# Inner feed-forward groups with the weight block stationary, and the row factor multiplied in by VectorE

## The chip, the cores and the metric

The kernel runs on one core of one Trainium2 chip. The metric is the device time of one execution in microseconds; the number given is the median over several runs. TensorE (PE in the profile) multiplies, ScalarE (ACT), VectorE (DVE) and GpSimd (POOL) do the elementwise work, and SyncE (SP) issues the transfers of the weights.

## The reference, cut to what matters

Three transformer blocks for 256 tokens with a model width of 1024, all in float32. The part that is changed is their feed-forward layers: four gated ones with an inner width of 2816, and one of another form with an inner width of 4096.

```python
def rms_norm(x, g):
    xf = x.astype(jnp.float32)
    y = xf * lax.rsqrt(jnp.mean(xf * xf, axis=-1, keepdims=True) + EPS)
    return (y * g.astype(jnp.float32)).astype(x.dtype)

def swiglu(h, w_gate, w_up, w_down):
    return (jax.nn.silu(h @ w_gate) * (h @ w_up)) @ w_down

# twice in each of the two layers of the first part (ffn0 to ffn3):
f = swiglu(rms_norm(x, g[0]), w_ffn_gate[layer, 0], w_ffn_up[layer, 0], w_ffn_down[layer, 0])
x = x + 0.5 * rms_norm(f, g[1])

# at the end of the second part (ff):
hn = rmsnorm(h, norm2_g[l])
h = h + jnp.square(jax.nn.relu(hn @ w_ff1[l])) @ w_ff2[l]
```

## The kernel before

**Three products for one.** The matmuls run in the type fp32r. Each operand is split in two parts, a rounded one (hi) and the remainder (lo), and a product is the sum of three matmuls: hi by hi, hi by lo, lo by hi (`mm3`, lines 573 to 577; the profile names these lines L575, L576 and L577). The 1.05 MB pieces of the weights arrive in four buffers `raw0` to `raw3` (SP, line 487). ScalarE writes `whi` (L1538) and VectorE writes `wlo` (L2155) from each of them; `used` tells that TensorE has read a piece for the last time, and so when its slot may be overwritten.

**x.** A normalisation is not applied to x: x is transposed unscaled except for the gain (which belongs to the rows of the weights), and lies as `xh` and `xl`, eight tiles of 128 rows by 256 tokens each. The factor of each token, 1/rms, is put in where sums are read out: as the tokens lie on the partitions there, it is a value per partition (`rcol`), which ScalarE's activation and VectorE's instruction take as their scale.

**Groups.** A gated layer is worked in 11 groups (`steps`) of 256 inner columns. The weights of the first product of a group are 512 columns, 256 of the gate and 256 of the up part, in two pieces `e0` and `e1` (the upper and the lower four tiles of 128 rows). In `x_half` a block of 128 tokens of `xh` or `xl` is the stationary operand and the 512 weight columns move past it: 8 tiles by 2 token blocks by 3 = 48 matmuls of 512 columns, with the sums in the two PSUM banks `GU`. ScalarE takes the silu of the gate part (L1649), VectorE multiplies by the up part (L2272) and writes `hid`, tokens on the partitions. The second product needs `hid` with its columns on the partitions, so TensorE transposes it (`hidden_transposes`, L768, 4 blocks of 128 by 128, float32) into the PSUM bank `TB`, from where ScalarE writes `hth` (L1638) and VectorE `htl` (L2265). The second product (`down`) is 2 tiles by 2 token blocks by 2 halves by 3 = 24 matmuls of 512 columns, added up in the four banks `DD`. The last layer, `ff`, has 8 groups of 512 inner columns; its sums go through relu (L1652) and a square (L2277), its transposes are 8, and its second product 48 matmuls.

**Order.** The order on every engine is written out by hand. On TensorE step g (function `step`, line 787) is: first half of the first product of group g, the transposes of group g-1, second half of the first product, second product of group g-1. ScalarE and VectorE do in the same step: the split of the second product's weights, `hth`/`htl` of group g-1, the split of `e0` of group g+1, the activation and product of group g, the split of `e1` of group g+1. Group 0 is done by token blocks in `head` (`first_head` in `ffn0`), the last group in `tail` or `tail2`, also by token blocks, so that their results are complete early. The groups between, 9 in each gated layer and 6 in `ff`, are called the inner groups here. Before step 1 of `ffn0` ScalarE also waits for two transposes of small parameters (L1498, L1499), which TensorE does in the middle of that step (`other_columns`).

Of the kernel before, what the change touches and what calls it, by code (L numbers as in the profile page):

```python
# [21 lines left out]
F32 = mybir.dt.float32  # L22
# [29 lines left out]
R_GKV, R_N1, R_N2, R_LB = 96, 104, 112, 120  # L52
R_PEK, R_PEV, R_SUB, R_HG, N_SM2 = 24, 40, 56, 57, 58
# [138 lines left out]
def two_blocks(nc, a, out, stop=None):  # L192
    ctx = ExitStack()
    with ctx:
# [14 lines left out]
        xh = sb("xh", [P, KT, S], F32R)  # L209
        xl = sb("xl", [P, KT, S], F32R)  # L210
# [55 lines left out]
        cols_ready = sem("cols_ready")  # L266
        out_ready, out_done, scaled, end_ready = sem("out_ready"), sem("out_done"), sem("scaled"), sem("end_ready")
# [44 lines left out]
        class Places:  # L312


            def __init__(self):
                self.next, self.gu, self.d, self.t, self.xh, self.hth = 0, 0, 0, [0, 0], 0, 0
                self.d0, self.x, self.h = 0, 0, 0
                self.gu0 = 0
# [10 lines left out]
        psc = sb("psc", [P, 2, 3 * P])  # L329
        lamv = small[:, 0:256].rearrange("p (i d) -> p i d", i=4)  # L330
# [238 lines left out]
        def _(pe):  # L569
# [179 lines left out]
            def ffn(name):  # L749
                steps, nd = ffn_shape(name)  # L750
                per, base, gu0 = 2 + nd, n.next, n.gu
# [3 lines left out]
                def hidden_ready(g, t, d=0):  # L755
                    if nd == 1:
                        pe.wait_ge(gu_used[t], d + gu0 + g + 1)
                    else:
                        pe.wait_ge(h_ready[t], d + sq0 + g + 1)

                def hidden_transposes(g, d):

                    for t in range(TT):
                        hidden_ready(g, t, d)
# [6 lines left out]

                def down(g, es, d, start):

                    for b, e in enumerate(es):
                        pe.wait_ge(t_used[b], d + t0[b] + g + 1)
# [11 lines left out]
                def step(g, at, d=0, static=True):  # L787

                    es = ent[at:at + per]
# [6 lines left out]
                    if name == "ffn0" and static and g == 1:  # L796
# [3 lines left out]
                    if name == "ffn0" and static and g == 1:  # L800
# [3 lines left out]
                def tail_transposes(g, t):  # L804

                    hidden_ready(g, t)
# [16 lines left out]
                def gate_tail(g, e0, e1):  # L823

                    for t in range(TT):
                        pe.wait_ge(gu_used[t], gu0 + g)
                    pe.wait_ge(lo_done[e0.slot], e0.raw_before + 1)
                    x_rows(gu_banks[0], e0, 0, 0)
                    hidden_transposes(g - 1, 0)
# [4 lines left out]
                def tail(g, at):  # L834
                    e0, e1, d0, d1 = ent[at:at + 4]
                    gate_tail(g, e0, e1)
                    pe.wait_ge(t_used[0], t0[0] + g)
                    tail_transposes(g, 0)
                    down_rows(d0, 0, 0)
                    pe.wait_ge(t_used[0], t0[0] + g + 1)  # L840
# [3 lines left out]
                    tail_transposes(g, 1)  # L844
                    down_rows(d0, 0, 1, range(1, 2)).then_inc(used[d0.slot], 1)
                    pe.wait_ge(t_used[1], t0[1] + 1)
                    n.t = [t0[0] + steps, t0[1] + 1]
# [6 lines left out]
                def tail2(g, at):  # L854
                    e0, e1, *ds = ent[at:at + 6]
                    gate_tail(g, e0, e1)
                    x_rows(gu_banks[1], e1, 1, 1).then_inc(used[e1.slot], 1)
                    for t in range(TT):
                        pe.wait_ge(t_used[t], t0[t] + g)
                    for t in range(TT):  # L860
# [4 lines left out]
                        tail_transposes(g, t)  # L865
                    for t in range(TT):
                        pe.wait_ge(t_used[t], t0[t] + g + 1)
# [2211 lines left out]
```

## Time and profile before

| what | value |
|---|---|
| time, median of 3 runs | 1379.26 us (1378.42 to 1379.76) |
| the profiled execution, first to last instruction (its span) | 1377.0 us |
| PE busy | 1359.0 us, 99% of the span, 6525 matmuls |
| PEld (weight loads) busy | 1116.0 us |
| DVE busy | 815.2 us, 59% |
| ACT busy | 681.7 us, 50% |
| POOL busy | 41.7 us, 3% |
| transfers | 247.09 MB, mean 179 GB/s |

The profile is of one execution on the chip. Its own time isn't printed beside its span; the median of the timed runs lies 2.3 us above the span, which is what lies around the first and the last instruction. The start of a row is more telling than its duration for TensorE, since matmuls overlap and their ends are modelled: the distance from one start to the next is what a matmul costs in a stream. A row of the timeline gives the start in us, the duration in us, engine, line, operation, output and inputs, the form and how many instructions were merged, and in brackets the idle time before and what ended it.

### The profile page before, as it was taken

The page shows a single profiled execution, that of the slowest core. Times are in us where ns is not written, and L with a number is a line of the kernel's source. Part 1 is how long each engine was busy: PE and PEld are TensorE (multiplying, and loading weights), DVE is VectorE, ACT ScalarE, POOL GpSimd, SP SyncE. Part 2 cuts the span into 40 slices and gives each one's busy share as a digit, 9 for nine tenths or more (in the row PEclk, how much of TensorE's full clock was granted, in tenths as well). Part 3 has the DMA queues.
Part 4 walks back from the last instruction along what each step waited for, and adds up shares of the span by engine and source line. Part 5 has one row for each costly group of instructions (what it writes and reads, how often), then busy time and mean ns, then how long its engine had stood idle before and what let it go on. Part 6 is the DMA issues. An engine that isn't in the chain of part 4 may idle for free.

```text
span 1377.0 us, 17411 instructions
## 1 busy us (share of the span) xinstructions
PE 1359.0 (99%) x6525; PEld 1116.0 (81%) x6525; DVE 815.2 (59%) x899; ACT 681.7 (50%) x875; POOL 41.7 (3%) x112
## 2 busy tenths in 40 slices
PE   8999999999999999999999999999999999999997
PEld 6888888888888888888887788888878778888886
DVE  5545567665555655554568855555767668654553
ACT  5444454464444554444467644444664466544442
POOL 3000000000000000000000100000000000000000
PEclk9999999999999999999999999999999999999999
DMA  8655656455556554655653265557444354565540
GB/s 294 210 192 191 222 166 217 159 165 193 185 183 215 197 183 139 192 188 183 230 182 108 93 199 193 188 183 240 163 178 153 104 175 141 191 219 190 178 166 31
DMA packets 160381, 247.09 MB, mean 179 GB/s; under 512 B 9103, under 2 KB 104649, under 8 KB 160329
## 3 DMA queue, kind: packets, MB, share of 16 engines
q1 hardware_dynamic: 160216, 246.33, 54.0%
q8 instruction: 35, 0.57, 0.2%
q14 instruction: 18, 0.14, 0.0%
q10 hardware_dynamic: 112, 0.05, 0.0%
HBM read 245.30 MB, written 1.05 MB: 179 GB/s over the span
## 4 chain that ended last, share of the span: by engine, by line
PE 97%; DVE 1%; ACT 1%; issue 0%; DMA 0%; POOL 0%; POOLq 0%; ACTq 0%; DVEq 0%
PE GU L575 15%; PE GU L577 15%; PE GU L576 15%; PE DD L575 12%; PE DD L577 12%; PE DD L576 12%; PE GU L640 4%; PE TB L612 3%; PE GU L647 2%; PE TB L768 2%; PE DD L1208 0%; PE GU L1473 0%; PE TB L1224 0%; PE GU L1476 0%; PE GU L1467 0%
## 5 line engine op out<-in xcount | busy, mean ns | idle before, releaser
L2155 DVE TENSOR_TENSOR wlo<-raw,whi 128x2048 fp32r<-128x2048 f32 x224 | 509.3, 2282 | 268.5 <-ACT whi L1538 268.3
L1538 ACT ACTIVATE whi<-raw 128x2048 fp32r<-128x2048 f32 x223 | 423.8, 1906 | 175.8 <-PE DD L577 167.9
L575 PE MATMUL GU<-whi,xh 128*128 128x512 f32 x928 | 367.3, 396 | 0.0
L577 PE MATMUL GU<-whi,xl 128*128 128x512 f32 x928 | 362.1, 390 | 0.0
L576 PE MATMUL GU<-wlo,xh 128*128 128x512 f32 x928 | 361.2, 389 | 0.0
L577 PEld LDWEIGHTS GU<-whi,xl 128*128 128x128 f32 x928 | 174.2, 188 | 37.3
L575 PEld LDWEIGHTS GU<-whi,xh 128*128 128x128 f32 x928 | 174.2, 188 | 35.4 <-issue 1.1
L576 PEld LDWEIGHTS GU<-wlo,xh 128*128 128x128 f32 x928 | 174.5, 188 | 34.5
L575 PE MATMUL DD<-whi,hth 128*128 128x512 f32 x496 | 194.8, 393 | 0.0
L577 PE MATMUL DD<-whi,htl 128*128 128x512 f32 x496 | 193.2, 390 | 0.0
L576 PE MATMUL DD<-wlo,hth 128*128 128x512 f32 x496 | 193.0, 389 | 0.0
L1638 ACT ACTIVATE hth<-TB 128x512 fp32r<-128x512 f32 x54 | 31.6, 599 | 165.0 <-PE TB L768 165.0
L577 PEld LDWEIGHTS DD<-whi,htl 128*128 128x128 f32 x496 | 93.1, 188 | 19.6
L576 PEld LDWEIGHTS DD<-wlo,hth 128*128 128x128 f32 x496 | 93.2, 188 | 18.8
L575 PEld LDWEIGHTS DD<-whi,hth 128*128 128x128 f32 x496 | 93.1, 188 | 18.7
L1649 ACT ACTIVATE sg<-GU,rs 128x256 f32<-128x256 f32 x88 | 41.8, 475 | 113.3 <-PE GU L577 106.5
L575 PE MATMUL DD<-whi,xh 128*128 128x512 f32 (+1 forms) x240 | 93.8, 391 | 0.1
L577 PE MATMUL DD<-whi,xl 128*128 128x512 f32 (+1 forms) x240 | 92.0, 383 | 0.0
L576 PE MATMUL DD<-wlo,xh 128*128 128x512 f32 (+1 forms) x240 | 92.0, 383 | 0.0
L2265 DVE TENSOR_TENSOR htl<-TB,hth 128x512 fp32r<-128x512 f32 x54 | 36.7, 690 | 89.8 <-ACT hth L1638 89.8
L2272 DVE SCALAR_TENSOR_TENSOR hid<-GU,rs,sg 128x256 f32<-128x256 f32 x88 | 42.3, 481 | 41.3 <-ACT sg L1649 41.2
L575 PEld LDWEIGHTS DD<-whi,xh 128*128 128x128 f32 x240 | 45.1, 188 | 9.1 <-DVE wlo L2155 0.5
(304 smaller groups left out, 1069.6 us busy)
## 6 DMA issues: line engine op xcount, KB each, us to landing
raw<-in_w_ffn_down SPq DMA_DIRECT2D x88, 512.0 KB, 4.2
raw<-in_w_ffn_gate SPq DMA_DIRECT2D x86, 512.0 KB, 4.0
raw<-in_w_ffn_up SPq DMA_DIRECT2D x86, 512.0 KB, 4.9
raw<-in_w_ff SPq DMA_DIRECT2D x64, 512.0 KB, 4.3
raw<-in_w_in SPq DMA_DIRECT2D x40, 512.0 KB, 4.5
raw<-in_w_conv_in SPq DMA_DIRECT2D x24, 512.0 KB, 4.8
raw<-in_w_kv SPq DMA_DIRECT2D x16, 512.0 KB, 4.8
raw<-in_w_conv_out SPq DMA_DIRECT2D x8, 512.0 KB, 4.7
```

What stands on the lines that cost most here:

```text
L575: pe.matmul(dst, h, w_h, start=start, stop=False)
L576: pe.matmul(dst, h, w_l, start=False, stop=False)
L577: return pe.matmul(dst, l, w_h, start=False, stop=stop)
L612: mm = pe.transpose(TB[0:m, bank, c:c + r], src, ident[0:r, 0:r])
L640: pe.matmul(dst[:, 0:m], xh[:, 4 * half + k, ts], view(w[e.slot], e)[:, k, :], start=(half == 0 and k == 0 and w is whi), stop=False)
L647: mm = pe.matmul(dst[:, 0:m], xl[:, 4 * half + k, ts], view(whi[e.slot], e)[:, k, :], start=False, stop=(half == 1 and k == 3))
L1538: nc.scalar.activation(whi[s][:, 0:size], raw[s][:, 0:size], ACT.Copy).then_inc(hi_done[s], 1)
L1638: nc.scalar.activation(hth[:, 2 * b:2 * b + 2, :].rearrange("p k n -> p (k n)"), TB[:, b, :], ACT.Copy).then_inc(hth_done[b], 1)
L1649: nc.scalar.activation(sg[:, t, 0:FG], GU[:, t, 0:FG], ACT.Silu, scale=rcol(pre, t)).then_inc(sg_done[t], 1)
L2155: nc.vector.tensor_tensor(wlo[s][:, 0:size], raw[s][:, 0:size], whi[s][:, 0:size].bitcast(F32), ALU.subtract).then_inc(lo_done[s], 1)
L2265: nc.vector.tensor_tensor(htl[:, 2 * b:2 * b + 2, :].rearrange("p k n -> p (k n)"), TB[:, b, :], hth[:, 2 * b:2 * b + 2, :].rearrange("p k ...
L2272: nc.vector.scalar_tensor_tensor(out=hid[:, t, 0:FG], in0=GU[:, t, FG:512], scalar=rcol(pre, t), in1=sg[:, t, 0:FG], op0=ALU.mult, op1=ALU ...
```

## The change

The first product of an inner group is turned round: a block of 128 rows by 128 weight columns is stationary, and x moves. `xh` and `xl` now lie in one tensor `xx`, so that one matmul of 512 columns has both parts of x move past a `whi` block (sums with xh in the first 256 columns of a bank, with xl in the other 256), and a second one of 256 columns has `xh` alone move past the `wlo` block, added to the first 256 columns. The sums come out with the inner columns on the partitions, so the transposes of these groups go. The four blocks of 128 columns fill four banks: `GU` (called pair 0, the gate) and now `TB` too (pair 1, the up part). `hidden_hi` and `hidden_lo` read `hid` instead of `TB` from group 1 on. ScalarE copies the xl halves of a pair to SBUF, VectorE adds the xh halves, multiplies by the row factor (now a value per column, so a row `rrow` that is the same on all partitions is needed), ScalarE takes the silu of pair 0 and VectorE makes the product. The row is made once for each layer: GpSimd spreads the factors over 128 columns (`rcols`), TensorE transposes these (`row_factors`), ScalarE copies the result. Group 0 and the last group stay as they are, except that fewer waits are needed.

```diff
-        xh = sb("xh", [P, KT, S], F32R)
-        xl = sb("xl", [P, KT, S], F32R)
+        xx = sb("xx", [P, 2, KT, S], F32R)
+        xh, xl = xx[:, 0, :, :], xx[:, 1, :, :]
...
+        def pair_of(p):
+            return (GU, TB)[p][:, :, :].rearrange("p a (u n) -> p a u n", u=2)
+        def both(t):
+            return t.rearrange("p (a n) -> p a n", a=2)
...
+                def row_factors():
+                    pe.wait_ge(rb_ready, n.rows + 1)
+                    for t in range(TT):
+                        mm = pe.transpose(DD[:, 2, t * P:(t + 1) * P], rcols[:, t, :], ident[:, :])
+                    mm.then_inc(row_t, 1)
+                def inner_part(e, half, pair, free=None):
+                    wh, wl = view(whi[e.slot], e), view(wlo[e.slot], e)
+                    for j in range(2):
+                        if free:
+                            pe.wait_ge(free[j], gu0 + 1)
+                        dst, cs = (GU, TB)[pair][:, j, :], slice((2 * pair + j) * P, (2 * pair + j + 1) * P)
+                        for k in range(4):
+                            kk = 4 * half + k
+                            pe.matmul(both(dst), wh[:, k, cs], xx[:, :, kk, :], start=(half == 0 and k == 0), stop=False)
+                            mm = pe.matmul(dst[:, 0:S], wl[:, k, cs], xh[:, kk, :], start=False, stop=(half == 1 and k == 3))
+                    return mm
-                    if g == 1:
-                        x_half(gu_banks, es[0], 0, 0, False, read=(gu_used, gu0 + 1), rows=True)
-                    else:
-                        for t in range(TT):
-                            pe.wait_ge(gu_used[t], d + gu0 + g)
-                        x_half(gu_banks, es[0], 0, 0, False, d=d)
-                    hidden_transposes(g - 1, d)
-                    x_half(gu_banks, es[1], 1, 4, True, d=d, done=gu_ready)
-                    down(g - 1, es[2:], d, start=(static and g == 1))
+                def step_1(at):
+                    e0, e1, *ds = ent[at:at + per]
+                    pe.wait_ge(lo_done[e0.slot], e0.raw_before + 1)
+                    inner_part(e0, 0, 0, gu_used)
+                    if name == "ffn0":
+                        other_columns()
+                    row_factors()
+                    first_transposes()
+                    pe.wait_ge(lo_done[e1.slot], e1.raw_before + 1)
+                    inner_part(e1, 1, 0).then_inc(w_ready, 1)
+                    for b in range(nd):
+                        pe.wait_ge(t_used[b], t0[b] + 1)
+                    inner_part(e0, 0, 1).then_inc(used[e0.slot], 1)
+                    inner_part(e1, 1, 1).then_inc(used[e1.slot], 1)
+                    pe.wait_ge(row_ready, n.rows)
+                    down(0, ds, 0, True)
+                def step(g, at, d=0):
+                    e0, e1, *ds = ent[at:at + per]
+                    pe.wait_ge(w_used[0], d + w0 + g - 1)
+                    pe.wait_ge(lo_done[e0.slot], d + e0.raw_before + 1)
+                    inner_part(e0, 0, 0)
+                    pe.wait_ge(w_used[1], d + w0 + g - 1)
+                    inner_part(e0, 0, 1).then_inc(used[e0.slot], 1)
+                    pe.wait_ge(lo_done[e1.slot], d + e1.raw_before + 1)
+                    inner_part(e1, 1, 0).then_inc(w_ready, 1)
+                    inner_part(e1, 1, 1).then_inc(used[e1.slot], 1)
+                    down(g - 1, ds, d, False)
...
+                def inner_low_sums(p, g, d):
...
+                    nc.scalar.activation(both(sg[:, p, :]), pair_of(p)[:, :, 1, :], ACT.Copy).then_inc(w_copied[p], 1)
+                def inner_gate(g, d):
+                    act.wait_ge(w_scaled[0], d + w0 + g)
+                    nc.scalar.activation(sg[:, 0, :], hid[:, 0, :], ACT.Silu).then_inc(w_gate, 1)
                     split(ent[e + nd], d)
-                    gate(g, d)
+                    inner_low_sums(0, g, d)
+                    if nd == 1:
+                        inner_gate(g, d)
+                    inner_low_sums(1, g, d)
                     split(ent[e + nd + 1], d)
...
+                def inner_sums(p, g, d):
...
+                    nc.vector.tensor_tensor(both(hid[:, p, :]), pair_of(p)[:, :, 0, :], both(sg[:, p, :]), ALU.add)\
+                        .then_inc(w_used[p], 1)
+                def inner_scales(p, g, d):
+                    nc.vector.tensor_tensor(both(hid[:, p, :]), both(hid[:, p, :]), rrow.unsqueeze(1).broadcast_to([P, 2, S]),
+                                            ALU.mult).then_inc(w_scaled[p], 1)
+                def inner_products(g, d):
+                    if nd == 1:
+                        nc.vector.tensor_tensor(hid[:, 0, :], hid[:, 1, :], sg[:, 0, :], ALU.mult).then_inc(w_hid[0], 1)
+                        return
+                    for p in range(2):
+                        nc.vector.scalar_tensor_tensor(out=hid[:, p, :], in0=hid[:, p, :], scalar=0.0, in1=hid[:, p, :],
+                                                       op0=ALU.max, op1=ALU.mult).then_inc(w_hid[p], 1)
                     split(ent[e + nd], d)
-                    hidden(g, d)
+                    inner_sums(0, g, d)
+                    inner_scales(0, g, d)
+                    inner_sums(1, g, d)
+                    inner_scales(1, g, d)
+                    inner_products(g, d)
                     split(ent[e + nd + 1], d)
...
+                nc.gpsimd.tensor_copy(rcols, rs[:, c:c + TT].unsqueeze(2).broadcast_to([P, TT, P])).then_inc(rb_ready, 1)
```

## Rows read from the trace of the kernel before

**Rows 1.** The page, busy time of each engine.
```profile
PE 1359.0 (99%) x6525; PEld 1116.0 (81%) x6525; DVE 815.2 (59%) x899; ACT 681.7 (50%) x875; POOL 41.7 (3%) x112
```
**Rows 2.** The page, the chain that ended last, by engine.
```profile
PE 97%; DVE 1%; ACT 1%; issue 0%; DMA 0%; POOL 0%; POOLq 0%; ACTq 0%; DVEq 0%
```
**Rows 3.** The waits of PE, the longest: sum, times, longest one.
```profile
PE DD L1503 <- DMA proj<-in_g_norm: 4.4, 1, 4.4
```
**Rows 4.** Windows: one inner step of ffn0, then no matmul at the end.
```profile
56.00:72.79 16.79, 16.79 (x78) 13.91 (x77) 8.45 (x6) 7.08 (x7) 0.00 (x0) 1.00 0.57 187
...
1370.00:1373.00 3.00, 0.00 (x0) 0.00 (x0) 2.28 (x3) 1.15 (x2) 0.59 (x2) 1.00 0.40 165
1373.00:1374.00 1.00, 0.00 (x0) 0.00 (x0) 0.55 (x1) 0.62 (x1) 0.14 (x1) 0.54 0.00 0
```
**Rows 5.** Timeline of PE around the transposes of an inner step of ffn0.
```profile
60.91 0.40 PE L577 MATMUL GU<-whi,xl 128*128 128x512 f32 x1
61.15 0.60 PE L768 MATMUL TB<-ident,hid 128*128 128x128 f32 x4
...
61.82 0.39 PE L576 MATMUL GU<-wlo,xh 128*128 128x512 f32 x1
```
**Rows 6.** The same in ff.
```profile
1226.81 0.40 PE L577 MATMUL GU<-whi,xl 128*128 128x512 f32 x1
...
1228.15 0.39 PE L576 MATMUL GU<-wlo,xh 128*128 128x512 f32 x1
```
**Rows 7.** Timeline of PE: fp32r matmuls of 280 columns, nine starts.
```profile
1128.06 0.29 PE L575 MATMUL DD<-whi,xh 128*128 128x280 f32 x1
...
1129.08 0.29 PE L577 MATMUL DD<-whi,xl 128*128 128x280 f32 x1
```
**Rows 8.** Timeline: four fp32r matmuls of 256 columns and their followers.
```profile
728.79 0.50 PE L1000 MATMUL DD<-hth 64*128 64x256 f32 x4 [0.25 <-ACT proj L1770]
...
729.14 0.82 PE L1004 MATMUL DD<-proj 64*128 64x128 f32 x7
```
**Rows 9.** Lines of PE: the transposes of hid.
```profile
L768 PE MATMUL TB<-ident,hid 128*128 128x128 f32 x216 | 31.2, 272 | 0.0
```
**Rows 10.** The page, costliest groups, two of DVE.
```profile
L2155 DVE TENSOR_TENSOR wlo<-raw,whi 128x2048 fp32r<-128x2048 f32 x224 | 509.3, 2282 | 268.5 <-ACT whi L1538 268.3
...
L2265 DVE TENSOR_TENSOR htl<-TB,hth 128x512 fp32r<-128x512 f32 x54 | 36.7, 690 | 89.8 <-ACT hth L1638 89.8
```
**Rows 11.** Timeline, ffn1: first matmul of step 1, last product of group 0.
```profile
301.70 0.39 PE L575 MATMUL GU<-whi,xh 128*128 128x512 f32 x1
...
303.27 0.48 DVE L2272 SCALAR_TENSOR_TENSOR hid<-GU,rs,sg 128x256 f32<-128x256 f32 x1
```
**Rows 12.** The same in ffn2, then in ffn3.
```profile
536.54 0.39 PE L575 MATMUL GU<-whi,xh 128*128 128x512 f32 x1
...
537.25 0.48 DVE L2272 SCALAR_TENSOR_TENSOR hid<-GU,rs,sg 128x256 f32<-128x256 f32 x1
...
795.23 0.39 PE L575 MATMUL GU<-whi,xh 128*128 128x512 f32 x1
...
796.73 0.48 DVE L2272 SCALAR_TENSOR_TENSOR hid<-GU,rs,sg 128x256 f32<-128x256 f32 x1
```
**Rows 13.** The same in ffn0, with the split of its first down weights and htl.
```profile
21.59 0.39 PE L575 MATMUL GU<-whi,xh 128*128 128x512 f32 x1
...
23.66 0.48 DVE L2272 SCALAR_TENSOR_TENSOR hid<-GU,rs,sg 128x256 f32<-128x256 f32 x1
...
27.78 1.92 ACT L1538 ACTIVATE whi<-raw 128x2048 fp32r<-128x2048 f32 x1
...
31.93 0.68 DVE L2265 TENSOR_TENSOR htl<-TB,hth 128x512 fp32r<-128x512 f32 x1
```
**Rows 14.** The same in ff: first matmul of step 1, and both htl.
```profile
1198.91 0.39 PE L575 MATMUL GU<-whi,xh 128*128 128x512 f32 x1
...
1206.05 1.28 DVE L2265 TENSOR_TENSOR htl<-TB,hth 128x512 fp32r<-128x512 f32 x2
```

More of the change, by code:

```diff
@@ L52 @@
 R_GKV, R_N1, R_N2, R_LB = 96, 104, 112, 120
+FFNS = ("ffn0", "ffn1", "ffn2", "ffn3", "ff")
 R_PEK, R_PEV, R_SUB, R_HG, N_SM2 = 24, 40, 56, 57, 58
@@ L266, in two_blocks @@
         cols_ready = sem("cols_ready")
+        rb_ready, row_t, row_ready = sem("rb_ready"), sem("row_t"), sem("row_ready")
+        w_ready, w_gate = sem("w_ready"), sem("w_gate")
+        w_copied, w_used, w_scaled, w_hid, w_low = ([sem(f"{x_}{i}") for i in range(2)] for x_ in (
+            "w_copied", "w_used", "w_scaled", "w_hid", "w_low"))
         out_ready, out_done, scaled, end_ready = sem("out_ready"), sem("out_done"), sem("scaled"), sem("end_ready")
@@ L317, in __init__ @@
                 self.d0, self.x, self.h = 0, 0, 0
-                self.gu0 = 0
+                self.w, self.rows = 0, 0
         def ffn_shape(name):
@@ L821, in down_rows, with gate_tail @@
                     return mm
-                def gate_tail(g, e0, e1):
-                    for t in range(TT):
-                        pe.wait_ge(gu_used[t], gu0 + g)
+                def gate_tail(e0, e1):
+                    pe.wait_ge(w_used[0], w0 + steps - 2)
                     pe.wait_ge(lo_done[e0.slot], e0.raw_before + 1)
                     x_rows(gu_banks[0], e0, 0, 0)
-                    hidden_transposes(g - 1, 0)
                     pe.wait_ge(lo_done[e1.slot], e1.raw_before + 1)
@@ L1630, in ffn @@
                 steps, nd = ffn_shape(name)
-                per, t0, gu0 = 2 + nd, list(n.t), n.gu
+                per, t0, gu0, w0 = 2 + nd, list(n.t), n.gu, n.w
+                n.rows += 1
                 base = seg[name]
@@ L1716, in ffn @@
                     hidden_hi(steps - 2, 0)
-                    gate(steps - 1, 0)
+                    for t in range(TT):
+                        gate_rows(1, t)
                     split(ent[e + 2])
@@ L2258, in ffn @@
                 steps, nd = ffn_shape(name)
-                per, gu0, sg0, hth0 = 2 + nd, n.gu, n.sg, n.hth
+                per, gu0, sg0, hth0, w0 = 2 + nd, n.gu, n.sg, n.hth, n.w
+                n.rows += 1
                 base = seg[name]
@@ L2333, in ffn @@
                     hidden_lo(steps - 2, 0)
-                    hidden(steps - 1, 0)
+                    for t in range(TT):
+                        dve.wait_ge(w_low[t], n.w if t == 0 else steps - 2)
+                        hidden_rows(1, t)
                     split(ent[e + 2])
@@ L3007, in norms, with row_columns @@
                     norm(1, ssq[:, c:c + 1], msq[:, c:c + 1], rs[:, c:c + 1], D, rs_ready)
+            def row_columns(name):
+                pre = {"ffn0": "pre0", "ffn1": "pre2", "ffn2": "pre4", "ffn3": "pre6", "ff": "pre8"}[name]
+                pool.wait_ge(rs_ready, order(pre))
+                c = ncol[pre]
+                if name != "ffn0":
+                    pool.wait_ge(row_t, FFNS.index(name))
+                nc.gpsimd.tensor_copy(rcols, rs[:, c:c + TT].unsqueeze(2).broadcast_to([P, TT, P])).then_inc(rb_ready, 1)
             chain(nc.gpsimd.memset(ident[:, :], 0.0))
@@ L3043, in _ @@
             ins.then_inc(const2, 1)
-            norms("pre0", "pre5")
+            norms("pre0", "pre0")
+            row_columns("ffn0")
+            norms("post0", "pre2")
+            row_columns("ffn1")
+            norms("post2", "pre3")
+            row_columns("ffn2")
+            norms("post3", "pre5")
             pool.wait_ge(rs_ready, order("pre5"))
```

170 lines of the change are left out of this document (98 added, 72 removed).

## The prediction

> **What bounds the kernel now.** I read the page's busy times first. TensorE is busy for 1359.0 us, 99% of the span, VectorE for 59%, ScalarE for 50% [rows 1]. A busy share near one isn't proof, so the chain that ended last comes next: 97% of it is TensorE [rows 2]. The waits say the same from the other side: the longest that TensorE ever had was 4.4 us for the first transfer [rows 3], and no wait inside a feed-forward layer is listed. The windows then give one inner step of a gated layer, 16.79 us, with TensorE busy throughout, VectorE for 8.45 and ScalarE for 7.08 us, transfers at 57%, the granted clock at 1.00 [rows 4]. So the kernel is a stream of matmuls. What the change is worth is read from distances between starts on TensorE, and only there, unless it makes TensorE wait.
>
> **Prices on TensorE.** An inner step has 72 matmuls of 512 columns and one block of four transposes. From the last matmul before the block to the second one behind it are 0.91 us [rows 5]. Two distances of plain matmuls lie in that. If one is w, then 72 w + (0.91 - 2 w) = 16.79, so w = 0.227 us, and the block costs 0.46 us. In ff the same two starts are 1.34 us apart [rows 6], so its block of eight costs 1.34 - 0.45 = 0.89. The difference, 0.43 for four more, puts one transpose at 0.108 us.
>
> The matmul of 256 columns is what decides. No full-height one in fp32r is in the trace. The nearest rows are those of 280 columns: nine starts, so eight distances, in 1.02 us, 0.1275 us each [rows 7]. Between 280 and 512 columns a column costs (0.227 - 0.1275) / 232 = 0.43 ns, so 256 columns come to 0.1275 - 24 x 0.00043 = 0.117 us. A second row bears it out: four fp32r matmuls of 256 columns on two halves of the rows, so two in sequence on each half, take 0.35 us from the first load to the start of the next kind [rows 8]. With one exposed load of about a transpose's distance taken off, 0.12 us each are left. I take 0.118. Bounds: not under 0.108, the distance of a transpose with its own load of 128 columns, and not over 0.1275, that of 280 columns.
>
> The Trainium skill (TensorE: Matmul & The Clock Gate, section "Back-to-back issue gap") has N / 2.4 + 2.5 ns for a warm matmul, 109 ns for 256 columns. For 512 columns it gives 216 ns, and the distance of 227 here says that it leaves out 11 ns in this stream [rows 5]; by its figure for 256 alone my forecast would be 12 us lower. The same page (section "LDWEIGHTS (loading the stationary operand)") has P / 1.2, 107 ns for a block of 128 columns. That speaks against the change: the loads are 64 for each first product instead of 48, and half of them have only a 256-column matmul to hide behind. By this rule it still fits into 118 ns, by 11.
>
> **What goes.** Of the 216 transposes of hid in `hidden_transposes` [rows 9] those of group 0 stay. Gone are nine blocks of 0.46 us in each of four layers, 16.6 us, and six of 0.89 in ff, 5.3 us. Sum: -21.9 us.
>
> **What comes on TensorE.** Two transposes for the row of factors in each of five layers, 10 x 0.108 = +1.1 us. The first product of an inner group is 32 matmuls of 512 columns and 32 of 256 instead of 48 of 512: the same number of columns, but sixteen more starts. There are 4 x 9 + 6 = 42 inner groups: 1344 x 0.118 - 672 x 0.227 = 158.6 - 152.5 = +6.1 us. By the bounds of the 256-column matmul this term is -7.4 to +18.9. That the moving operand now has two pieces far apart I cost at nothing: the matmuls of [rows 8] read a repeated operand in two pieces.
>
> **What comes on VectorE and ScalarE.** Per gated step VectorE loses 0.69 + 2 x 0.48 and gains hidden_lo from SBUF, two sums, two scalings and one product of 512 columns, each taken as the htl row, 0.69 [rows 10]: 3 x 2.28 + 6 x 0.69 = 11.0 us of a step of 16.5. I followed the order through a step that starts at 0. Split of the down weights done at 4.4, htl at 5.1; e0 is released at 5.52 and split until 9.9; pair 0 of the sums is complete at 8.28, read out and added by 10.6, scaled 11.3; pair 1, complete at 11.04, is added by 13.2, scaled 13.9, product 14.6, split of e1 until 16.8. TensorE wants pair 0's banks at 16.5, pair 1's at 19.2, the split e1 at 22.0, and htl of this group at 27.5. Every slack is over 5 us, so both engines stay hidden, at a cost of nothing. If each elementwise pass took twice 0.69, e1 would still be 1 us early. In ff VectorE has 4 x 2.28 + 8 x 0.69 = 14.6 of 21.9 us. Transfers move the same bytes, the weight buffers come free at nearly the same points, and the transfers of such a step take 57% of their engines' time [rows 4]. The row itself: GpSimd's copy starts once the factors are there, some 5 us before TensorE gets to it, and it has 3% to do [rows 1]. ScalarE's copy of it is 0.2 to 0.7 us in a slack of 5 us.
>
> **What comes as waits.** Step 1 of each layer has a new order, and this is where I expect TensorE to stand still.
> - Bank j = 1 of `GU` is wanted 6 distances earlier: after half of pair 0's first part, 4 x (0.227 + 0.118) = 1.38 us from the step's start, instead of 2.72. It comes free when group 0's second product ends on VectorE, plus some 0.06 us for the signal. In ffn1: free at 303.27 + 0.48 + 0.06 = 303.81, wanted at 301.70 + 1.38 = 303.08, a wait of 0.7 [rows 11]. In ffn2 537.79 against 537.92, none; in ffn3 797.27 against 796.61, 0.7 [rows 12]. In ffn0 24.20 against 22.97, 1.2 [rows 13]. In ff ScalarE frees it, early enough. Together 2.6 us.
> - `TB` is now a bank for sums. Pair 1 of step 1 may start only when htl of group 0 has been made from it. Before, that was due at the second product, two quarters later. In ffn0 pair 1 is reached at 24.20 + 1.38 + 0.4 (parameters) + 0.22 (row) + 0.46 + 2.76 = 29.4, and htl ends at 31.93 + 0.68 = 32.6 [rows 13], since the split of the down weights, begun at 27.78 behind the parameter columns, comes first on both engines. TensorE gets to the columns 1.5 us earlier than before, so if the weights had landed the wait would shrink by that; the transfers of this stretch are dense, and I take them as landing about when the split began. Wait: 3.2 (bounds 1.6 and 3.2). In ff it is reached at 1198.91 + 2.76 + 0.22 + 0.89 + 2.76 = 1205.5, and the second htl ends at 1206.05 + 1.28 = 1207.4 [rows 14], behind two splits in VectorE's queue: 1.9. In ffn1 to ffn3 one split stands ahead and htl is done about a microsecond early. Together 5.1 us.
> - No clock is lost: at the end the granted clock is at 1.00, 2.4 GHz, through 3 us with no matmul at all, and falls in the next slice [rows 4]. The longest wait is 3.2 us. If it did fall, the stretch behind would run at 1.2 GHz, and some 2 to 3 us more would go.
> - In the tail the transposes of the last group come 0.46 us earlier. VectorE then has two splits, htl and the product to do in 8.2 us, which by the durations above ends at 7.6. Nothing, at most 0.5 us in each layer.
>
> **Sum.** -21.9 + 1.1 + 6.1 + 2.6 + 5.1 = -7.0 us. The profiled span of 1377.0 becomes 1370; the median lies 2.3 us above its span, so 1379.3 becomes 1372.3.
>
> **Rivals.**
> - A, the waits don't come, because group 0's work on VectorE and ScalarE moves forward with TensorE: only the steady terms stay, -14.7, 1364.6 us. Against it: the products and the splits that are waited for hang on the head and on transfers, which don't change.
> - B, the 256-column matmul runs at its lower bound: 1344 x 0.010 less, 1358.9 us with the waits. For it: transposes load as many columns in 0.108. Against it: [rows 8] and the line through 280 and 512.
> - C, slower than before: the 256-column matmul is bound by the weight load ahead of it and goes no faster than the 280-column one. At 0.1275, 1344 x 0.0095 = 12.8 more, 1385.1 us. The point from which it decides is 0.118 + 7.0 / 1344 = 0.123 us, halfway between my value and the bound. For it: no row has 256 full-height columns in fp32r, and loads take turns with matmuls of two lengths. If a load really held TensorE for the 0.171 us that its busy time comes to (1116.0 / 6525 [rows 1]), it would be 1344 x 0.053 = +71 us, but 280 columns at 0.1275 exclude that.
> - D, the change doesn't hide where it should: VectorE's chain is longer than I have it and holds back pair 0's banks in each of 42 groups. A quarter microsecond in each would be +10, 1383. Against it are 5 us of slack.
>
> **Chances.** The forecast with its own spread (1368 to 1376.5) 0.52; A 0.12; B 0.08; C 0.15; D or another new wait 0.05; in between forecast and C, with a matmul at 0.121 to 0.124 or longer waits, 0.08. A measurement of this kernel tells a difference from none at about 0.2%, 2.8 us. Faster by more: the first three, 0.72. Within it: 0.12. Slower: 0.16. The range reaches from A, 1363, to 1383, short of C: below lies most of B, above about half of C.
>
> **What would show it.** In the profile after: starts of the first product alternate between 0.227 and 0.118 us; an inner step of a gated layer takes 16.5 us against 16.79, one of ff 21.9 against 22.7; the 192 transposes of hid are gone; PE's waits list VectorE at step 1 of ffn0 and ff with about 3 and 2 us; VectorE is busy for some 110 us more. Wrong would be a distance above 0.123 behind a 256-column matmul, a wait in every inner step, or a granted clock below 1.00 after 32 us.

## The result and the profile after

| | before | after |
|---|---|---|
| median of the timed runs | 1379.46 us (1378.42 to 1379.76, 4 runs) | 1386.83 us (1386.15 to 1387.81, 4 runs) |
| span of the profiled execution | 1377.0 us | 1384.3 us |
| time of that execution | not printed | 1386.2 us |

The changed kernel is slower: the ratio after to before is 1.0056 [1.0044, 1.0068]. The forecast was 1372.3 us and its range ended at 1383, so the forecast missed by 14.5 us and had the wrong sign. Between the spans lie +7.3 us where I had -7.0.

The page after, busy time of each engine, answers to [rows 1]. Below it stands the chain that ended last, answering to [rows 2].

```profile
PE 1359.5 (98%) x7015; PEld 1133.5 (82%) x7015; DVE 912.4 (66%) x1031; ACT 710.1 (51%) x916; POOL 44.1 (3%) x117
...
PE 94%; DVE 2%; ACT 2%; SPq 1%; DMA 1%; issue 0%; POOL 0%; POOLq 0%; ACTq 0%; DVEq 0%
```

The kernel is still a stream of matmuls, and VectorE got its 97 us (110 forecast) without leading the chain. PE's busy time is the number to stop at: 192 transposes have gone, worth 21.9 us, and it did not fall (1359.0 to 1359.5). Something in the stream costs as much as they did.

The waits of PE after (sum, times, longest) answer to [rows 3]. The first is the old one for the first transfer.

```profile
PE DD L1558 <- DMA proj<-in_g_norm: 4.4, 1, 4.4
PE TB L803 <- DVE htl L2345: 4.2, 2, 2.5
PE GU L803 <- DVE hid L2351: 2.1, 3, 1.0
...
PE GU L1522 <- DVE whi L3061: 1.1, 1, 1.1
```

The rows of L803 are the two new waits of step 1, 6.3 us, where I had 5.1 and 2.6.

Next, one inner step of ffn0. This row of the windows after answers to the first of [rows 4].

```profile
79.54:96.33 16.79, 16.79 (x89) 14.30 (x88) 10.76 (x10) 7.88 (x7) 0.00 (x0) 1.00 0.58 187
```

The step takes 16.79 us, as before, not 16.5. There is no wait in it, the clock is at 1.00, and the transfers take 58% (57% before). So in the steady state of a gated layer the change gives nothing, though a block of 0.46 us has gone from each step. In ff, where the block that goes is 0.89 us, it gives something. The windows between two starts of the second product there are, before and after:

```profile
1233.40:1256.09 22.69, 22.69 (x105) 18.84 (x104) 11.76 (x9) 9.91 (x8) 0.00 (x0) 1.00 0.56 186
...
1243.45:1265.69 22.24, 22.24 (x115) 18.82 (x113) 14.17 (x13) 9.80 (x8) 0.00 (x0) 1.00 0.57 189
```

That is 0.45 us a step, where 0.8 was forecast. The timeline of PE inside the step of ffn0 shows why. This is the first product of the inner group, which answers to [rows 5].

```profile
79.88 0.40 PE L803 MATMUL GU<-xx,whi 128*128 128x512 f32 x1
80.11 0.28 PE L804 MATMUL GU<-xx,wlo 128*128 128x256 f32 x1
80.23 0.40 PE L803 MATMUL GU<-xx,whi 128*128 128x512 f32 x1
80.47 0.28 PE L804 MATMUL GU<-xx,wlo 128*128 128x256 f32 x1
...
80.94 0.40 PE L803 MATMUL GU<-xx,whi 128*128 128x512 f32 x1
```

From 79.88 to 80.94 are three pairs in 1.06 us, 0.353 us a pair. My sum had 0.227 + 0.118 = 0.345. A pair divides into 0.117 (0.11 to 0.12) behind the start of the short matmul, as forecast, and 0.236 (0.23, then 0.24) behind the start of the long one, which I had left at 0.227. So the excess shows beside the short matmul and not on it.

It also outlasts the group. The second product behind it, which the change doesn't touch, starts like this in the kernel after:

```profile
74.04 0.40 PE L589 MATMUL DD<-whi,hth 128*128 128x512 f32 x1
74.28 0.40 PE L590 MATMUL DD<-wlo,hth 128*128 128x512 f32 x1
74.52 0.40 PE L591 MATMUL DD<-whi,htl 128*128 128x512 f32 x1
74.75 0.40 PE L589 MATMUL DD<-whi,hth 128*128 128x512 f32 x1
```

These distances are 0.24, 0.24 and 0.23; after about ten matmuls they are back at 0.227, and 0.06 us has been lost by then. From 74.04 to the next step's start at 79.54 the second product takes 5.50 us, 24 x 0.2267 + 0.06. Of the 16.79 that leaves 11.29 for the 32 pairs of the first product, 0.3528 each, as the three pairs above say.

Where the time went over the whole kernel:

| term | forecast | found after |
|---|---|---|
| transposes of hid gone | -21.9 | -21.9 |
| row of factors, 10 transposes | +1.1 | +1.1 |
| first product: 1344 pairs at 0.3528 less 2016 x 0.2267 | +6.1 | +17.1 |
| second product, its first matmuls late, 42 x 0.061 | 0 | +2.6 |
| waits for `GU` and for htl | +7.7 | +6.3 |
| clock at half behind the wait in ffn0 | 0 | +1.6 |
| step 1 of ffn0 begins later | 0 | +1.0 |
| sum | -7.0 | +7.8 (measured +7.3) |

The two transposes of a row take 0.22 us up to the next kind's start, as priced (0.28 in ffn0). The clock's term is five pairs that took 3.35 us (33.25 to 36.60) instead of 1.76. The later start of step 1 in ffn0 (22.58 instead of 21.59) has two parts in the timelines: the wait ahead of the head's first matmul of 512 columns grew from 0.54 to 1.08, and such matmuls followed each other at 0.425 us, as the half clock gives, until 12.5 us instead of 11.1, which costs another 0.4. The sum is 0.5 us above what was measured; that part I can't place.

### The profile page after: what moved, and what is told of

The parts are those of the page before. It is cut to its first block, busy times and chain, and to the rows that moved or that the text cites. A ratio compares the mean times of both kernels' runs of the same rounds, so it can differ in the third digit from the quotient of the medians.

```text
span 1384.3 us, 18651 instructions
## 1 busy us (share of the span) xinstructions
PE 1359.5 (98%) x7015; PEld 1133.5 (82%) x7015; DVE 912.4 (66%) x1031; ACT 710.1 (51%) x916; POOL 44.1 (3%) x117
## 4 chain that ended last, share of the span: by engine, by line
PE 94%; DVE 2%; ACT 2%; SPq 1%; DMA 1%; issue 0%; POOL 0%; POOLq 0%; ACTq 0%; DVEq 0%
PE DD L589 12%; PE DD L591 12%; PE DD L590 12%; PE TB L803 11%; PE GU L803 11%; PE TB L804 6%; PE GU L804 5%; PE GU L589 4%; PE GU L591 4%; PE GU L590 4%; PE GU L654 4%; PE TB L626 3%; PE GU L661 2%; DVE wlo L2232 1%; ACT whi L1593 1%; DMA raw<-in_w_ffn_down 1%
## 5 line engine op out<-in xcount | busy, mean ns | idle before, releaser
L803 PE MATMUL TB<-xx,whi 128*128 128x512 f32 x672 | 242.4, 400 | 4.2 <-DVE htl L2345 4.2
L803 PE MATMUL GU<-xx,whi 128*128 128x512 f32 x672 | 241.3, 399 | 2.1 <-DVE hid L2351 2.1
L804 PE MATMUL TB<-xx,wlo 128*128 128x256 f32 x672 | 189.3, 282 | 0.0
L804 PE MATMUL GU<-xx,wlo 128*128 128x256 f32 x672 | 188.8, 281 | 0.0
L803 PEld LDWEIGHTS TB<-xx,whi 128*128 128x128 f32 x672 | 127.0, 189 | 36.4 <-DVE htl L2345 4.8
L803 PEld LDWEIGHTS GU<-xx,whi 128*128 128x128 f32 x672 | 126.2, 188 | 33.1 <-DVE hid L2351 3.0
L804 PEld LDWEIGHTS GU<-xx,wlo 128*128 128x128 f32 x672 | 126.9, 189 | 1.6
L804 PEld LDWEIGHTS TB<-xx,wlo 128*128 128x128 f32 x672 | 127.8, 190 | 0.0
L589 PE MATMUL GU<-whi,xx 128*128 128x512 f32 x256 | 101.1, 395 | 0.0
L591 PE MATMUL GU<-whi,xx 128*128 128x512 f32 x256 | 99.9, 390 | 0.0
L589 PE MATMUL DD<-whi,xx 128*128 128x512 f32 (+1 forms) x240 | 93.9, 391 | 0.0
L591 PE MATMUL DD<-whi,xx 128*128 128x512 f32 (+1 forms) x240 | 92.1, 384 | 0.0
```

Of the source, the lines that this page charges most:

```text
L589: pe.matmul(dst, h, w_h, start=start, stop=False)
L591: return pe.matmul(dst, l, w_h, start=False, stop=stop)
L803: pe.matmul(both(dst), wh[:, k, cs], xx[:, :, kk, :], start=(half == 0 and k == 0), stop=False)
L804: mm = pe.matmul(dst[:, 0:S], wl[:, k, cs], xh[:, kk, :], start=False, stop=(half == 1 and k == 3))
```

## The experiments

The expectations name four theories of the 0.353 us. **L** (layout): the moving operand, read from two pieces 2048 columns (8 KB) apart, is slow by itself. **R** (rhythm): the change between two lengths costs it as such. **S** (short slot): a matmul of 256 columns can't quite cover the load of 128, and a run of short ones would show that on themselves. **K**, from e5 on: the load that falls into the short slot comes late, and the lateness is passed on to the long matmuls behind. All diffs are against the changed kernel. "Step" is the distance between the starts of the second product in successive inner steps of ffn0 (16.79 in the kernel after).

**e1, the two parts of x side by side.**

```diff
-xx = sb("xx", [P, 2, KT, S], F32R)
-xh, xl = xx[:, 0, :, :], xx[:, 1, :, :]
+xx = sb("xx", [P, KT, 2, S], F32R)
+xh, xl = xx[:, :, 0, :], xx[:, :, 1, :]
...
-pe.matmul(both(dst), wh[:, k, cs], xx[:, :, kk, :], ...)
+pe.matmul(both(dst), wh[:, k, cs], xx[:, kk, :, :], ...)
```

> The changed kernel with xx laid out [P, KT, 2, S], so that the moving operand of the 512-column matmul is one contiguous piece. In the changed kernel a pair of a 512- and a 256-column matmul takes 0.353 us (0.236 + 0.117) where 0.345 was forecast. Theory L (layout: a moving operand of two pieces 8 KB apart costs 10 ns at each 512-column matmul): the pair falls to 0.344, 1344 pairs, 12 us less, 1375 us. Rival R (rhythm: matmuls of two lengths in turn cost it, whatever the layout): the pair stays at 0.353 and the time at 1387 us.

Measured: 1384.42 us (1383.77 to 1386.12), ratio 1.0041 [1.0027, 1.0055]. The timeline of PE in e1, the same place in a step:

```profile
79.15 0.40 PE L803 MATMUL GU<-xx,whi 128*128 128x512 f32 x1
...
80.21 0.40 PE L803 MATMUL TB<-xx,whi 128*128 128x512 f32 x1
```

Three pairs lie between these two rows, again in 1.06 us, and the step is 16.79. Theory L falls. The 2.4 us between the two medians are no more than what differs in ffn0: the wait for htl was 1.7 us instead of 2.5, the clock didn't fall there (1.6), and the wait for whi was 0.6 instead of 1.1.

**e2, the short matmuls in runs of four.**

```diff
 for k in range(4):
     pe.matmul(both(dst), wh[:, k, cs], xx[:, :, 4 * half + k, :], ...)
+for k in range(4):
     mm = pe.matmul(dst[:, 0:S], wl[:, k, cs], xh[:, 4 * half + k, :], ...)
```

> The changed kernel with the matmuls of each block of 128 columns in another order: the four of 512 columns one after the other, then the four of 256. Theory R: the cost sits at the change of length, eight changes in eight matmuls become two, so the 512-column distance falls to about 0.227 to 0.230 and three quarters of 12 us go: 1378 us. Rival S (the short matmul: a 256-column slot can't quite cover the load of 128 columns and its issue, and the backlog shows at its neighbour): four in a row show it openly as a distance of about 0.126, and the sum and the time stay, 1387 us. Theory L: the 512-column distance stays at 0.236, 1387 us.

Measured: 1381.09 us (1380.26 to 1382.14), ratio 1.0012 [1.0003, 1.0022]; the step is 16.69. The timeline of PE in e2, where a row with x4 is a run of four:

```profile
78.86 1.09 PE L802 MATMUL GU<-xx,whi 128*128 128x512 f32 x4
79.79 0.63 PE L804 MATMUL GU<-xx,wlo 128*128 128x256 f32 x4
80.26 1.09 PE L802 MATMUL TB<-xx,whi 128*128 128x512 f32 x4
```

From 78.86 to 79.79 four long ones take 0.93 (0.2325 each), and from 79.79 to 80.26 four short ones 0.47 (0.1175 each). The same matmuls in another order save 0.1 us a step, so the price isn't a constant of either kind of matmul. But it doesn't sit at the changes of length alone either. At 0.2267 and 0.117 throughout, the step would be 16.44. With a quarter of the changes 0.25 of the 0.35 us above that are left, where R had counted on a quarter (1378 us), and S's 0.126 in a run of four doesn't appear.

**e3, no short matmul.** It adds the term low times low to the inner groups.

```diff
-mm = pe.matmul(dst[:, 0:S], wl[:, k, cs], xh[:, kk, :], ...)
+mm = pe.matmul(both(dst), wl[:, k, cs], xx[:, :, kk, :], ...)
```

> The changed kernel with the second matmul of each pair as long as the first: the lo part of the weights meets both parts of x, so one more term is added up (lo by lo) and all matmuls have 512 columns and a two-piece moving operand. It is slower by the 256 columns more in each of 1344 matmuls; it is read by its distances. Theory L: all distances 0.236, about 1387 + 1344 x 0.119 = 1547 us. Rivals R and S: 0.227 as in the kernel before, about 1387 + 1344 x 0.101 = 1522 us.

Measured: 1512.56 us in one run; R and S had 1522. Of the 9 us less, some 7 are the waits for htl and `GU`, here 1.2 instead of 6.3, and a clock that didn't fall in ffn0. The timeline of PE in e3:

```profile
79.25 0.39 PE L803 MATMUL TB<-xx,whi 128*128 128x512 f32 x1
79.48 0.39 PE L804 MATMUL TB<-xx,wlo 128*128 128x512 f32 x1
79.70 0.39 PE L589 MATMUL DD<-whi,hth 128*128 128x512 f32 x1
```

Every distance is 0.227, and the step is 88 x 0.2267 = 19.95. A moving operand in two pieces costs nothing in an even stream. This speaks against L a second time, and it shows that the second product loses nothing when there are no short matmuls ahead of it.

**e5, load half as many columns.** Both blocks of the inner groups have 64 columns, so half of the sums' rows are left out. The columns streamed stay the same.

```diff
-pe.matmul(both(dst), wh[:, k, cs], ...)
+pe.matmul(both(dst[0:64, :]), wh[:, k, cs.start:cs.start + 64], ...)
```

(and the same for `wl`)

> The changed kernel with the stationary blocks of the inner groups cut from 128 to 64 columns: half of the inner columns' sums are left out, the lengths of the moving operands stay 512 and 256. Layout is out as a cause (one piece: same distances), and with equal lengths (all 512) the distance is 0.227. Left are K (the load of 128 columns, some 0.107 us, fills the slot of a 256-column matmul, and what is late there is passed on to the next 512-column ones) and R (unequal lengths as such). K: with half the load the pair falls from 0.353 to 0.344, 1375 us. R: 0.353 and 1387 us.

Measured: 1367.72 us in one run, 19 us less than after; the step is 16.35. The timeline of PE in e5:

```profile
79.07 0.39 PE L803 MATMUL GU<-xx,whi 128*64 128x512 f32 x1
79.30 0.27 PE L804 MATMUL GU<-xx,wlo 128*64 128x256 f32 x1
79.41 0.39 PE L803 MATMUL GU<-xx,whi 128*64 128x512 f32 x1
```

A pair takes 0.34 us (0.228 and 0.112), and the second product runs at 0.227 from its third matmul on: 32 x 0.340 + 24 x 0.2267 = 16.32. R had 0.353 and falls as the whole cause: the lengths alternate as before. K had 0.344 and 1375 us, so more than the late part has gone. The short matmul too fell below its 0.117. The edit halves two things at once, the columns loaded and the columns that a matmul then works with; which of them counts isn't separated here or in e9 and e10. The waits for htl (4.1 us) were still there, so these 19 us have nothing to do with them.

**e6, short matmuls of 384 columns.** The sums aren't the kernel's. If a load simply needs more time than the slot beside it has, as K says, a wider slot cures it.

```diff
-mm = pe.matmul(dst[:, 0:S], wl[:, k, cs], xh[:, kk, :], ...)
+mm = pe.matmul(dst[:, 0:384].rearrange("p (a n) -> p a n", a=2), wl[:, k, cs], xx[:, :, kk, 0:192], ...)
```

> The changed kernel with the short matmul of each pair at 384 columns instead of 256 (192 columns of each part of x; the sums are not those of the kernel). K: the slot is now wider than a load, so nothing is late, the pair is 0.227 + 0.172 = 0.399 us, about 1387 + 1344 x 0.046 = 1449 us. R: the 0.009 us of the unequal lengths stay, 0.408 us and 1461 us.

Measured: 1452.54 us in one run; the step is 18.45. The timeline of PE in e6:

```profile
82.28 0.40 PE L803 MATMUL GU<-xx,whi 128*128 128x512 f32 x1
82.52 0.34 PE L804 MATMUL GU<-xx,wlo 128*128 128x384 f32 x1
82.69 0.39 PE L803 MATMUL GU<-xx,whi 128*128 128x512 f32 x1
...
83.10 0.40 PE L803 MATMUL GU<-xx,whi 128*128 128x512 f32 x1
```

A pair is 0.407 to 0.41. Along the line of the forecast, 384 columns are 0.172 and a pair would be 0.399, so 8 ns stay at a slot half as wide again. That is R's 0.408 and not K's 0.399. The 0.172 is a point between 280 and 512 columns that no even stream here measures; the long matmul's part doesn't hang on it, 0.24 in the first row here and 0.232 on average instead of 0.227. The simple form of K, a slot narrower than a load, isn't enough.

**e9 and e10, which load.** In the inner groups seven of eight blocks of the high part (e9) or of the low part (e10) have 64 columns, so part of the sums is left out. The block with 128 is the first of a sum in e9 and the last in e10.

```diff
+a_, b_, c0 = (64 if half or k else P), P, cs.start               # e9
+a_, b_, c0 = P, (64 if k < 3 or not half else P), cs.start       # e10
+pe.matmul(both(dst[0:a_, :]), wh[:, k, c0:c0 + a_], ...)
+mm = pe.matmul(dst[0:b_, 0:S], wl[:, k, c0:c0 + b_], ...)
```

> The changed kernel with 64-column stationary blocks for whi alone (seven of eight; the first of a sum stays at 128), wlo at 128. The load of a whi block runs during the 256-column matmul ahead of it. With both blocks at 64 a pair took 0.340 us (0.228 + 0.112); at 384 columns instead of 256 the 0.008 us above the lengths stayed, so a slot narrower than a load isn't the whole cause. K (the load that falls into the short slot is what is late): seven of eight pairs at about 0.340, an inner step of about 16.4 us, 1370 us. If the load of wlo, in the long slot ahead of the short matmul, is what costs: pairs stay at 0.353, 16.8 us, 1387 us.

> The same the other way round: 64 columns for wlo alone (seven of eight), whi at 128. K: no change, pairs at 0.353, 1387 us. The other way: 0.340 and 1370 us. If both loads share the cost: about half of it in each of the two runs.

Measured, one run each: e9 1369.50 us, e10 1380.35. The timelines of PE, first of e9, then of e10:

```profile
80.17 0.39 PE L804 MATMUL GU<-xx,whi 128*64 128x512 f32 x1
80.40 0.28 PE L805 MATMUL GU<-xx,wlo 128*128 128x256 f32 x1
...
80.85 0.40 PE L804 MATMUL TB<-xx,whi 128*128 128x512 f32 x1
...
81.20 0.39 PE L804 MATMUL TB<-xx,whi 128*64 128x512 f32 x1
```

```profile
83.88 0.39 PE L804 MATMUL TB<-xx,whi 128*128 128x512 f32 x1
84.11 0.28 PE L805 MATMUL TB<-xx,wlo 128*64 128x256 f32 x1
...
85.61 0.39 PE L804 MATMUL GU<-xx,whi 128*128 128x512 f32 x1
```

e9: from 80.17 to 80.85 two pairs in 0.68, 0.340 each, step 16.39. e10: from 83.88 to 85.61 five pairs in 1.73, 0.346 each, step 16.62. The row at 80.85 is the one in eight whose whi block has 128 columns: up to 81.20 its pair takes 0.35, beside 0.34 for the others of the same trace. Whi's block is loaded while the matmul of 256 columns runs: in the kernel after a load of it starts at 25.52, the short matmul beside it at 25.51. Halving that load removes 0.40 us a step, 12.5 ns a pair. That is nearly all that e5 removed (0.44), and more than the 0.3 by which the step had missed the forecast. Halving wlo's, loaded while the 512 columns run, removes 0.17, 5 ns a pair. K had expected nothing from it, and "both share the cost" a half in each run, so neither form is right as it was put: whi's load alone nearly suffices, and wlo's has a smaller part.

**e4, the order of group 0's work.** On ScalarE and VectorE, hth and htl of group 0 go ahead of the split of its down weights.

```diff
+if g == 1:
+    hidden_lo(0, d)
 for q in range(nd): split(ent[e+q], d)
-hidden_lo(g - 1, d)
+if g > 1:
+    hidden_lo(g - 1, d)
```

(and the same with `hidden_hi` on ScalarE)

> The changed kernel, with hth and htl of group 0 made ahead of the split of the down weights on ScalarE and VectorE, in step 1 alone. The waits of TensorE for htl at TB (4.2 us in ffn0 and ff) go, and with the first of them the 3.4 us at half clock behind it in ffn0, which cost 1.6 us: 5.8 us less, 1381 us. If the waits only move to the down weights, whose split is now later, the time stays at 1387 us.

Measured: 1379.83 us (1379.08 to 1380.6), ratio 1.0004 [0.9994, 1.0013]. Seven of the 7.4 us are back, 5.8 were expected. The windows of e4 over the place of the wait:

```profile
28.00:32.00 4.00, 4.00 (x24) 3.43 (x24) 2.58 (x2) 2.34 (x3) 0.00 (x0) 1.00 0.96 308
32.00:36.00 4.00, 4.00 (x25) 3.49 (x24) 1.07 (x2) 2.40 (x2) 0.00 (x0) 1.00 0.59 194
```

PE has no idle time and the clock stays at 1.00. Of the 7.0 us the waits for htl are 4.2, the clock 1.6 and a shorter wait for whi 0.6. So this wait, with what it pulls behind it, is worth about as much as the whole difference between the two kernels. The forecast had already counted 5.1 us for it, though. Without the slow pairs the kernel would be the faster one despite the wait, as e9 shows (1369.50 with 4.1 us of it, though with part of the sums left out).

**e7, runs of 16.** All 16 long matmuls of a half, then its 16 short ones, in steps 2 and on; step 1 has the runs of four of e2.

```diff
-inner_part(e0, 0, 0)
-inner_part(e0, 0, 1).then_inc(...)
+for pair in range(2):
+    inner_hi(e0, 0, pair)
+inner_low(e0, 0, 0)
+inner_low(e0, 0, 1).then_inc(...)
```

> The kernel of the grouped order with longer runs in steps 2 and on: sixteen matmuls of 512 columns, then sixteen of 256, for each of e0 and e1. After a short matmul the next eleven of 512 columns are late by 0.061 us together (in the second product of the changed kernel), in a run of four by about 0.022. From eight runs of four to two of sixteen: 8 x 0.022 - 2 x 0.061 = 0.05 us less in each step, 16.64 instead of 16.69, 2 us in all, 1379 us. If lateness hangs on the number of short matmuls and not on the runs, nothing changes: 1381 us.

Measured: 1376.99 us (1375.57 to 1378.81), ratio 0.9983 [0.9973, 0.9992]. The timeline of PE in e7:

```profile
81.79 1.11 PE L820 MATMUL GU<-xx,wlo 128*128 128x256 f32 x8
82.74 1.12 PE L820 MATMUL TB<-xx,wlo 128*128 128x256 f32 x8
83.70 1.32 PE L811 MATMUL GU<-xx,whi 128*128 128x512 f32 x5
```

Sixteen short ones take 1.91 us. Here each is 0.119, more than the 0.117 in a pair, but their followers are late only once in 16. The step is 16.57, where 16.64 was expected: of the 0.35 us above 16.44, 0.13 are left with a sixteenth of the changes of length.

**e8 and e11, runs and the early deadlines together.** e8 is e2 with e4; in ffn1 to ffn3 VectorE also works off group 0's row product one split earlier. e11 is e7 with the same, and in step 1 the row of factors (in ffn0 the parameter columns too) is made between bank 0 and bank 1 of `GU`, which gives bank 1 more time.

```diff
-split_to(base + 4)
-hidden_rows(0, 1)
+split_to(base + 3)        # ffn1 to ffn3
+hidden_rows(0, 1)
+split_to(base + 4)
...
-inner_part(e0, 0, 0, gu_used)                   # e11
...
-row_factors()
+inner_part(e0, 0, 0, gu_used, ([other_columns] if name == "ffn0" else []) + [row_factors])
```

> Grouped order, hth and htl of group 0 first in step 1, and on VectorE the product of group 0's second token block ahead of the last split before it in ffn1 to ffn3. The parts add up if they are independent: 1387 - 5.7 (grouped) - 7.0 (htl early) - 1.1 (waits of ffn1 and ffn3 for GU) = 1373 us, 0.4% under the kernel before. If the moved split makes TensorE wait for e1 of step 1 instead, 1374.

> All that helped in one kernel: runs of sixteen in steps 2 and on, runs of four in step 1, hth and htl of group 0 first, the product of group 0's second token block ahead of a split in ffn1 to ffn3, and in step 1 the transposes of the parameters and of the row factors between the two banks of GU, to fill part of the wait there. From 1377.0 (runs of sixteen alone) less 7.0 less 1.1 less 0.6: 1368 us, 0.8% under the kernel before.

Measured: e8 1374.16 us (1373.7 to 1375.12), ratio 0.9963 [0.9948, 0.9977]. e11 1369.64 us (1369.15 to 1370.3), ratio 0.9931 [0.9918, 0.9945], against 1379.25 of the kernel before on the same chip. The waits of PE in e11:

```profile
PE DD L1579 <- DMA proj<-in_g_norm: 4.6, 1, 4.6
PE TB L626 <- ACT hid L1983: 1.7, 1, 1.7
PE GU L1543 <- DVE whi L3093: 0.9, 1, 0.9
```

Both new waits are gone from the head of the list (0.4 us for `GU` is left), and the step stays at 16.57. This version leaves nothing out of the change or of the computation, and it is 0.7% faster than the kernel before.

## Why the prediction was wrong

**The step that failed** is in "What comes on TensorE": "the same number of columns, but sixteen more starts", 1344 x 0.118 - 672 x 0.227 = +6.1. It was +17.1, and +19.7 with what falls on the second product. The price of the short matmul had bounds, and with them the term reached +18.9, but the long one beside it had none. The range ended at 1383, short of C's 1385.1, the case with the short one at its upper bound. The 0.118 was right (0.117). The 0.227 beside it, taken from an even stream of 512 columns, was not: in a stream of both kinds it is 0.236. I read [rows 7] and [rows 8] only inside runs of equal matmuls and never at their edges. Yet the edge was in the trace of before, in the matmuls of 512 columns behind the run of 280. This is PE's timeline there:

```profile
1140.57 0.40 PE L575 MATMUL GU<-whi,xh 128*128 128x512 f32 x1
...
1142.87 0.39 PE L576 MATMUL GU<-wlo,xh 128*128 128x512 f32 x1
```

Ten distances take 2.30 us, 0.230 each and not 0.227. Some 30 ns lost once in a stage is nothing. The 13.6 us missing from the forecast are 10 ns at each of 1344 pairs, a third of that. That the edge in before and the pairs after lose by the same mechanism is argued from their likeness, not shown.

**Rival C** had the right sign, and nearly the right number (1385.1), by a mechanism close to what e9 shows. It named "loads take turns with matmuls of two lengths", but then put the price on the 256-column matmul and wanted 0.1275 there. What I named as decisive, a distance above 0.123 behind a 256-column matmul, never appeared, while the pair as a whole passed C's point: 0.3528 is 0.345 + 0.008, and my C decided at 0.345 + 0.005. Had the price been set on pairs, C would have been the right case; as it stands, its nearness in time is in part luck.

**"No clock is lost"** failed as well. I leaned on one place, 3 us without a matmul at the end of before at 1.00 [rows 4]. PE's timeline after, at the wait in ffn0:

```profile
33.25 0.80 PE L803 MATMUL TB<-xx,whi 128*128 128x512 f32 x1 [2.46 <-DVE htl L2345]
...
34.06 0.63 PE L803 MATMUL TB<-xx,whi 128*128 128x512 f32 x1
```

And the windows of the same stretch, where the third number from the end is the granted clock:

```profile
31.00:33.00 2.00, 0.00 (x0) 0.00 (x0) 2.00 (x2) 0.02 (x1) 0.00 (x0) 1.00 0.80 257
33.00:34.00 1.00, 0.75 (x2) 0.66 (x3) 0.19 (x1) 0.00 (x0) 0.00 (x0) 0.58 0.36 77
34.00:36.00 2.00, 2.00 (x9) 1.71 (x8) 0.00 (x0) 0.00 (x0) 0.00 (x0) 0.50 0.94 328
36.00:37.00 1.00, 1.00 (x6) 0.85 (x6) 0.00 (x0) 0.00 (x0) 0.00 (x0) 0.72 0.81 332
37.00:39.00 2.00, 2.00 (x14) 1.72 (x13) 0.00 (x0) 1.08 (x1) 0.00 (x0) 1.00 0.02 6
```

Through the idle stretch itself 1.00 is shown. It falls as the matmuls come back, to 1.2 GHz for some 3.4 us, and costs about 1.6 us. That is less than the 2 to 3 I had put as the price if it fell.

**What held.** The waits came where I had put them, at htl and at the second bank of `GU`, with 6.3 us for 7.7. In ffn0 htl was waited for 1.7 us (e1, e2), 1.9 (e7) and 2.5 (after), inside my bounds of 1.6 and 3.2; in ff 1.7 in after, where my starts give 1.8 (I wrote 1.9). Rival A (no waits) falls with that. Rival B falls: no stretch shows 0.108 from a short matmul to its follower. VectorE and ScalarE stayed hidden in the steady state, as the step without a wait shows, so D falls too. The transposes were worth about their 21.9: the steps of ffn0 and ff leave no other number for them.

**What stays open.** Shown is that the stream is late where whi's block has 128 columns and the matmul beside its load has 256: e9 halves the block and the loss goes, with lengths, order and layout as they were. That it is the loading of the 128 columns, and not the work with them, is argued: in an even stream of 512 columns blocks of 128 cost nothing beyond 0.227 (e3). Not shown is what the load meets there. Why 384 columns still lose 8 ns a pair, why the loss falls more slowly than the number of changes of length (e2, e7), why wlo's load has a part (e10), why up to ten matmuls behind are late, and why 0.230 to 0.233 each is the rate at which they recover, no run here tells apart. The wait ahead of the head's first product in ffn0, part of the later start of step 1, differs between the versions (0.5 in before and e4, 0.6 in e1, 1.1 in after, 1.7 in e2), and I didn't trace why.

## What to carry to other kernels

Price a matmul in the stream that it will stand in. Take the distance over a whole period, neighbours included, and where the trace has the two lengths side by side only once, read that edge. If short matmuls with full-width weight blocks can't be avoided, put them in long runs: here 1, 4 and 16 in a row gave steps of 16.79, 16.69 and 16.57 us for the same work.

When a bank gets a second use or is wanted earlier, list its new earliest deadline in the first round, where the pipeline is still filling. The wait for htl was cured by changing the order of lines on the engines that were hidden, for 7.0 us (e4), and most of the one for `GU` in e11.

## What the hardware did that I had not expected

- Alternating 512 and 256 columns with blocks of 128 loaded for each costs 0.353 us a pair. With 64 columns in whi's block alone it is 0.340, with 64 in wlo's alone 0.346.
- Short matmuls are a little slower in a long run (0.119 in e7) than between long ones (0.117); the loss then stands on themselves instead of on their neighbours.
- The clock fell to half behind idle stretches of TensorE of 1.95 us (e7), 2.3 (e5, e9), 2.46 (after) and 3.0 (e10), and not behind 1.6 (e6) and 1.7 (e1, e2); yet at the end of before it was at 1.00 through 3.0 us without a matmul [rows 4]. Half clock lasted 3.4 us in the kernel after, and longer in e10, whose windows show (the clock is again the third number from the end):

```profile
34.00:36.00 2.00, 2.00 (x7) 1.31 (x6) 0.00 (x0) 0.00 (x0) 0.00 (x0) 0.50 1.00 377
36.00:38.00 2.00, 2.00 (x7) 1.31 (x6) 0.00 (x0) 0.00 (x0) 0.00 (x0) 0.50 0.27 111
```

So the length of an idle stretch alone doesn't tell here whether the clock falls, nor for how long.
